# One gathered tile's rows spread over more chunks, and a short convolution read from PSUM, in a two-layer decoder trunk

## The reference, cut to what matters

```
xn = rms_norm(x);  lru_in, fox_qkv, ..., gate_in = split(xn @ w_in)
y  = causal depthwise convolution of lru_in, 4 taps:  y = xp[:, 0:S]*w[0] + b;  y += xp[:, k:k+S]*w[k]
r  = sigmoid(y @ wa + ba);  i = sigmoid(y @ wx + bx)            # blocks of 128
a  = exp(-8 r softplus(-lam));  u = sqrt(1 - a*a) * (i * y)
h  = scan: h[t] = a[t] h[t-1] + u[t]                            # ya
x  = x + (g0*(ya@Wa) + g1*(yb@Wb) + g2*(yc@Wc)) @ w_out         # yb forgetting attention, yc mLSTM

hn = rms_norm(x);  q = hn @ wq                                  # 8 heads, 2 halves of 128
s1, s2 = q1 @ sub1.T, q2 @ sub2.T;  v1,i1 = top16(s1);  v2,i2 = top16(s2)
top_s, pos = top16(all 256 sums v1+v2);  idx = i1*128 + i2      # 16 of 16384 experts per head
act = gelu(dot(u_tab[idx], hn));  x = x + sum softmax(top_s) * act * v_tab[idx]
```

## Time and profile before

| | us |
|---|---|
| median of 3 runs (lowest, highest) | 4760.27 (4757.66, 4764.66) |
| the profiled execution | 4777.11 |
| its span, first to last instruction | 4775.3 |
| PE busy / PEld / DVE / ACT / POOL | 4448.6 / 3691.8 / 3138.8 / 1810.5 / 2693.7 |
| granted TensorE clock, mean | 0.972 |

### The profile page before, as it was taken

The page is one execution under the profiler, slowest core; times in us unless marked ns, Lnnn a source line. Parts: engine busy times, 40 slices in busy tenths (PEclk is TensorE's granted clock), DMA queues, the critical chain, the costliest instruction groups (busy, mean ns, idle before and its releaser), DMA issues.

```text
span 4775.3 us, 73532 instructions
## 1 busy us (share of the span) xinstructions
PE 4448.6 (93%) x21322; PEld 3691.8 (77%) x21322; DVE 3138.8 (66%) x5007; ACT 1810.5 (38%) x3307; POOL 2693.7 (56%) x1477
## 2 busy tenths in 40 slices
PE   7999999999999998999989999999999898889998
PEld 5766775789889897777767667757898898877776
DVE  5754223448889776888867541244488897668888
ACT  2234114124566652333332341231245666533333
POOL 5743663665456675555558436636654566655554
PEclk9999999999999999999999999999999999999999
DMA  3211221224689999999822112212246899999997
GB/s 105 80 49 36 80 81 47 70 78 137 182 259 283 298 318 329 335 343 333 292 87 84 49 36 83 79 42 75 80 142 192 260 288 302 335 315 343 340 338 268
DMA packets 467060, 891.87 MB, mean 187 GB/s; under 512 B 45600, under 2 KB 324640, under 8 KB 463776
## 3 DMA queue, kind: packets, MB, share of 16 engines
q1 hardware_dynamic: 387424, 617.22, 40.1%
q0 software_dynamic: 73728, 268.47, 16.2%
q10 hardware_dynamic: 5696, 3.85, 0.3%
HBM read 786.61 MB, written 102.76 MB: 186 GB/s over the span
## 4 chain that ended last, share of the span: by engine, by line
PE 61%; DVE 12%; issue 11%; DMA 8%; POOL 3%; ACT 3%; SPq 1%; DVEq 0%; ACTq 0%; POOLq 0%; another core or an unknown queue 0%
PE pair L824 6%; DMA ring<-v_tab 5%; PE bank L1230 5%; PE bank L824 5%; PE bank L1235 5%; PE bank L1225 4%; PE bank L1173 4%; PE bank L850 3%; PE pair L850 3%; PE pair L826 3%; PE bank L826 3%; PE bank L990 2%; PE bank L1177 2%; DMA ring<-u_tab 2%; DVE qk L2329 1%
## 5 line engine op out<-in xcount | busy, mean ns | idle before, releaser
L678 POOL TENSOR_TENSOR w_hi<-ring,ones 128x1024 fp32r<-128x1024 f32 x272 | 536.4, 1972 | 844.8 <-PE bank L850 277.8
L666 POOL TENSOR_TENSOR w_lo<-ring,w_hi 128x1024 fp32r<-128x1024 f32 x256 | 615.8, 2406 | 539.8 <-ACT w_hi L1628 532.3
L1173 PE MATMUL bank<-xT,w_hi 128*128 128x384 f32 x2048 | 720.3, 352 | 40.0 <-ACT gst L1640 36.4
L681 POOL TENSOR_TENSOR w_lo<-ring,w_hi 128x1024 fp32r<-128x1024 f32 x272 | 693.8, 2551 | 21.3
L1173 PE MATMUL bank<-xl_peer,w_hi 128*128 128x384 f32 x2048 | 698.8, 341 | 0.0
L1634 ACT CAST w_hi<-ring 128x1024 fp32r<-128x1024 f32 x252 | 266.0, 1056 | 671.7 <-PE bank L1235 445.3
L1628 ACT CAST w_hi<-ring 128x1024 fp32r<-128x1024 f32 x256 | 269.6, 1053 | 598.6 <-DVE ring L2297 427.8
L2389 DVE TENSOR_TENSOR cl<-att,ch 128x384 fp32r<-128x384 f32 x256 | 354.8, 1386 | 172.6 <-ACT ch L1699 165.6
L672 POOL TENSOR_TENSOR w_lo<-ring,w_hi 128x1024 fp32r<-128x1024 f32 x126 | 301.8, 2395 | 280.5 <-ACT w_hi L1634 280.5
L1173 PEld LDWEIGHTS bank<-xT,w_hi 128*128 128x128 f32 x2048 | 397.3, 194 | 43.1 <-ACT w_hi L1628 34.6
L1225 PE MATMUL bank<-w_hi,ch 128*128 128x512 f32 x1524 | 392.1, 393 | 21.4 <-ACT ch L1699 21.4
(11 more groups left out here) (360 smaller groups left out, 9332.8 us busy)
## 6 DMA issues: line engine op xcount, KB each, us to landing
ring<-v_tab SPq DMA_DIRECT2D x252, 512.0 KB
ring<-w_stream SPq DMA_DIRECT2D x240, 512.0 KB
ring<-u_tab SPq DMA_DIRECT2D x512, 128.0 KB
g_spill<-gst SPq DMA_DIRECT2D x256, 192.0 KB
hn<-u_tab SPq DMA_DIRECT2D x256, 128.0 KB
x_last<-u_tab SPq DMA_DIRECT2D x256, 128.0 KB
w_spill<-vg SPq DMA_DIRECT2D x12, 2048.0 KB
w_spill<-att SPq DMA_DIRECT2D x12, 2048.0 KB
```

The costliest lines, as they stand in the source:

```text
L666: nc.gpsimd.tensor_tensor(w_lo[s % 2][:, :], ring[2 + s % 2][:, :], w_hi[s % 2][:, :].bitcast(F32), ALU.subtract)\
L678: nc.gpsimd.tensor_tensor(w_hi[b][:, 0:n], src, ones[:, 0:1].to_broadcast([P, n]), ALU.mult)\
L681: nc.gpsimd.tensor_tensor(w_lo[b][:, 0:n], src, w_hi[b][:, 0:n].bitcast(F32), ALU.subtract)\
L1173: nc.tensor.matmul(out, w_hi[s % 2][:, c * P:(c + 1) * P], dense_parts(c)[part], start=(c == 0 and part == 0), stop=False)
```

## The change

Two edits that don't touch each other.

**LRU.** ACT reads the slot from PSUM and makes the last tap (`last_tap`); DVE adds the other three from the same PSUM bank, slot by slot, shifted by 1, 2 and 3 columns; `xpad` is gone, the bank is drained when the third is added. `xc` and `TI` have a buffer for each block. FZ now comes before FV in the order of weights, and gate products 1 stand between slots 1 and 2 of FZ.

**The gathered tile.** In each of the first three query rounds DVE also does the last tile's best 16 of 256 sums for the round's two heads (`sparse_heads`), in place of doing it for all heads in UE. The experts of the first four heads follow in chunks 2 to 6 of UE, those of the rest in chunks 24 to 31; tile 0's choice moves to chunks 7 to 23 and tile 1's to 32 to 54. Gathers begin at chunk 8 and dots at chunk 12: 8 in chunks 11 to 23, 112 in 24 to 119, 8 in 120 to 127. 38 of the 128 dots (the first 8, then every fourth) are taken by two engines: POOL multiplies the row by the token's vector, of which DVE puts a copy in SBUF (`nwb`), and ACT sums (`row_sum`).

```diff
-ROWS = [0] * (4 * LEAD + 14) + shares(18, 18) + shares(40, 32) + shares(54, 32) + shares(16, 8) \
+ROWS = [0] * 11 + shares(8, 4 * LEAD - 11) + shares(112, 4 * WROUNDS) + shares(8, 8) \
     + [0] * 4 + shares(SLOTS, NCHUNK - 4)
+SHARED_ROWS = [n for n in range(SLOTS) if n < FIRST_ROW[4 * LEAD] or n % 4 == 3]
-        xc = merged[:, 0:4, :]
-        TI = og[:, 0:4, :]
+        xc = [merged[:, 0:4, :], yT[:, 4:8, :]]
+        TI = [og[:, 0:4, :], merged[:, 0:4, :]]
...
+            def row_times(L, n):
+                if n == SHARED_ROWS[0]:
+                    pool.wait_ge(row_ready.sem, row_ready.at(L, "N2", 0, 1))
+                pool.wait_ge(g_ready[n % NG], landed(L, n))
+                stand(pool)
+                nc.gpsimd.tensor_tensor(grow[n % NG], grow[n % NG], nwb[:, :], ALU.mult).then_inc(row_product.sem, 1)
...
                     if c < NCHUNK:
                         expert_low(L, c // 4, c % 4)
+                        for m in shared_rows(c):
+                            row_times(L, m)
-                    if c == 4 * LEAD + 11:
-                        pool.wait_ge(eidx_ready.sem, eidx_ready.at(L, "T", 0, 2))
+                    if c == 8:
+                        pool.wait_ge(eidx_ready.sem, eidx_ready.at(L, "T", 0, 1))
...
-                project_tokens(L, "FV", 0, of_tile(xT), xl_of_tile)
-                gate_products(1, range(2))
-                values = tokens_beside(L, "FV", 1, of_tile(xT), xl_of_tile, 24)
-                for _ in range(3):
-                    next(values)
-                gate_products(1, range(2, 4))
-                next(values)
-                values.close()
                 for s in range(4):
                     project(L, "FZ", 0, s, x_parts(xl_mix))
+                    if s == 1:
+                        gate_products(1)
+                for i in range(2):
+                    project_tokens(L, "FV", i, of_tile(xT), xl_of_tile)
...
-                def conv_input(i, s):
+                def last_tap(i, s):
+                    k = 4 * i + s
                     proj_wait(L, "LRU", i, s)
-                    nc.scalar.copy(xpad[:, 4 * i + s, CONV - 1:], bank[s][:, :]).then_inc(drained_sem[s], 1)
+                    nc.scalar.activation(xc[i][:, s, :], bank[s][:, :], ACT.Identity, scale=pcol("conv_w", (CONV - 1) * KC + k),
                                          bias=pcol("conv_b", k)).then_inc(tap_ready.sem, 1)
...
+                def row_sum(n):
+                    act.wait_ge(row_product.sem, row_product.at(L, "U", 0, shared_at(n)))
+                    nc.scalar.activation(grow[n % NG], grow[n % NG], ACT.Copy, accum_out=actv[:, n:n + 1])\
+                        .then_inc(row_summed.sem, 1)
...
+                def conv(i, s):
+                    k = 4 * i + s
+                    dve.wait_ge(tap_ready.sem, tap_ready.at(L, "LRU", i, s + 1))
+                    for back in range(1, CONV):
+                        ins = V.scalar_tensor_tensor(out=xc[i][:, s, back:], in0=bank[s][:, 0:SEQ - back],
+                                                     scalar=pcol("conv_w", (CONV - 1 - back) * KC + k), in1=xc[i][:, s, back:],
+                                                     op0=ALU.mult, op1=ALU.add)
...
+                        c = Chain(dve, heads_step, L, "WQ", i)
+                        for _ in sparse_heads(c, lambda j: slice_of(tv_s, i, j), lambda j: slice_of(posu_s, i, j)):
+                            pass
...
+                V.tensor_copy(nwb[:, :], pair[:, :]).then_inc(row_ready.sem, 1)
+                sooner, later = 1 + 8, 5 + 6 + 8 + 1
+                pieces = [[0] * 5 + shares(upto, 16) + [1], shares(sooner, 5)]
```

More of the change, by code:

```diff
@@ L1678, in _ @@
                     expert_high(0, s)
-                with act.Fori(0, LEAD - 2) as i:
+                with act.Fori(0, 2) as i:
                     round_of(i)
+                stand(act)
+                with act.Fori(0, 1):
+                    for i in range(2, LEAD - 1):
+                        round_of(i)
                 soft(0, wts)
-                round_of(LEAD - 2)
                 round_of(LEAD - 1, tile=0)
@@ L1690, in _ @@
                         round_of(LEAD + 8 * d + y, k=8 * d + y, tile=DENSE if y < 7 else d + 1)
-                with act.Fori(LEAD + WROUNDS, ROUNDS["UE"] - 1) as i:
-                    round_of(i)
+                stand(act)
+                with act.Fori(0, 1):
+                    for i in range(LEAD + WROUNDS, ROUNDS["UE"] - 1):
+                        round_of(i)
                 round_of(ROUNDS["UE"] - 1, last=True)
@@ L1887, in decay @@
                     dve.wait_ge(drained_sem[7], drained[7].at(L, "LRU", i, 2))
-                    dve.wait_ge(conv_done.sem, conv_done.at(L, "LRU", i, 4))
-                    ins = V.scalar_tensor_tensor(out=TI, in0=TI, scalar=1.0, in1=xc, op0=ALU.add, op1=ALU.mult)
+                    for s in range(4):
+                        dve.wait_ge(drained_sem[s], drnd(L, "LRU", i) + 2)
+                    ins = V.scalar_tensor_tensor(out=TI[i], in0=TI[i], scalar=1.0, in1=xc[i], op0=ALU.add, op1=ALU.mult)
                     if i == 0:
@@ new lines, in sparse_heads @@
+                def sparse_heads(c, best, where):
+                    v = kval.rearrange("p (h a t) n -> p t h a n", a=2, t=TT)[:, SP_T, :, :, :]
+                    both = cand[:, 0:2, :]
+                    pair_of = [P, 2, TOPK, TOPK]
+                    c.step(V.tensor_tensor(both.rearrange("p h (a b) -> p h a b", a=TOPK),
+                                           v[:, :, 0, :].unsqueeze(3).to_broadcast(pair_of),
+                                           v[:, :, 1, :].unsqueeze(2).to_broadcast(pair_of), ALU.add))
+                    c.wait()
+                    stand(dve)
+                    yield
+                    for n in range(2):
+                        for j in range(2):
+                            c.step(V.max(best(j)[n], both[:, j, :]))
+                        c.wait()
+                        stand(dve)
+                        yield
+                        for j in range(2):
+                            c.step(V.max_index(where(j)[n], best(j)[n], both[:, j, :]))
+                        c.wait()
+                        stand(dve)
+                        yield
+                        if n == 0:
+                            for j in range(2):
+                                c.step(V.match_replace(both[:, j, :], best(j)[n], both[:, j, :], NEG * 1e8))
+                            c.wait()
+                            stand(dve)
+                            yield
@@ new lines, in _ @@
+                for i in range(LAST):
+                    stand(dve)
+                    with dve.Fori(0, 1):
+                        c = Chain(dve, dve_step, L, "WQ", i)
+                        keys_wait(i)
+                        for _ in best_keys(c, i, 0, TT):
+                            pass
+                        dve.sem_inc(best_done.sem, 1)
+                        c.close()
+                        stand(dve)
+                        c = Chain(dve, heads_step, L, "WQ", i)
+                        for _ in sparse_heads(c, lambda j: slice_of(tv_s, i, j), lambda j: slice_of(posu_s, i, j)):
+                            pass
+                        c.close()
+                        stand(dve)
@@ L2366, in _ @@
                     for _ in range(ROWS[n]):
-                        dot(used)
+                        if used not in SHARED_ROWS:
+                            dot(used)
                         used += 1
@@ L2404, in _ @@
                     if n == 4:
-                        for _ in sparse_choice:
+                        for _ in second:
                             pass
```

294 lines of the change are left out of this document (162 added, 132 removed).

## The result

The changed kernel takes 4786.3 us (median of five runs, 4776.8 to 4794.4) against 4760.2 for the kernel before: a ratio of 1.0053, with a 95% interval of 1.0036 to 1.0071. It is slower by half a per cent; 4680 was forecast, with a range of 4630 to 4742. The profiled execution took 4794.4 with a span of 4792.5, 17.2 more than before.

The account below looks back on a forecast made before the run. PE is busy 4448.6 of 4775.3 us, so gains are PE's waits, in UE for DVE, later loads. 2 x 12.5 (LRU) - 2 x 4.5 (query rounds) + 35 + 29 (UE) = 80 us off 4760: 4680, range 4630 to 4742.

Parts of the forecast that it names:

- search 1 begins 1.2 us late and search 2 2.4: Query rounds: 6 us of heads against 4.78 us idle delay the searches; loss 4.5 us a layer, from 3 to 15.
- Chunks 54 to 87: 7 forecast: UE: DVE's sum of 5.29 us a chunk is over by 0.2, 7 us lost in layer 1, from 0 to 14.
- Behind a row product stands the next w_lo ... So I cost them at nothing there.: UE's weights chunks: POOL needs 4.4 and ACT 3.9 of 5.08 us a chunk, so shared rows cost PE nothing.
- Slower: Rival, UE: POOL and ACT wait on each other, shared rows hold w_lo beyond its cover; +100 us, 4860; chance 0.09.
- 1.05 us a row on: UE: the cost per shared row from which the slower rival decides, 76 rows against 80 us gained.
- 5 us of cover: UE's weights chunks: w_lo may be about 5 us late before PE notices.
- 2.4 us a row: UE, the slower rival: each row holding w_lo too long costs PE its product again; 76 x 2.4 = 182 us.
- 15 us a layer named for a thinner cover: UE's weights chunks: 0.5 us for each of 30 rows if w_lo's cover is thinner than taken.
- A chunk costs DVE's sum plus 0.35 us of small waits.: UE's weights chunks: DVE's work plus 0.35 us sets a chunk's time where that exceeds 5.08 us.
- the one at 25: UE, chunks 24 to 31: the start of the weights steps costs 5.5 us as before, within 15 forecast.
- the 1824 and 1557 KB a chunk: UE, chunks 88 to 119: loads per chunk before and after, put at 359 and 306 GB/s; the window moved 316.
- The rule weighed in the prediction: DVE with two SBUF inputs and GpSimd reading SBUF share ports in turn; if offloading didn't help, about 4740.

Follow-up runs that it names:

- e3_sum_first: The changed kernel with ACT's sum of a shared row put ahead of w_hi of the same step instead of behind it; ratio 0.9922 to the kernel before.
- e2_unshared: The changed kernel with only the first 8 rows shared, all 112 rows of the weights chunks being DVE's dots; ratio 0.9959 to the kernel before.
- e11_no_subtract: The changed kernel without DVE's subtraction of the maximum in the dense tiles' softmax, exp reading the scores themselves; ratio 1.0018 to the kernel before.

## Why the prediction was wrong, step by step

**LRU: right.** 12.5 us a layer forecast, 11.0 and 12.4 measured; the taps at 0.75 for 0.69, and the splits of POOL are late next.

**Query rounds: the mechanism right, the size half.** The work of the heads was sized well (6). The step that failed is "search 1 begins 1.2 us late and search 2 2.4": I set 6 against an idle time of 4.78 and left out the gaps around the heads (1.0 before the next search, 0.3 ahead), and a sum that can meet a split (2.46 us in place of 0.69). It cost 9.9 us in place of 4.5.

**UE: wrong, and here is nearly all of the miss,** 90 of the 97 us between the forecast gain of 80 and the 17 lost by the profiles. By its parts: chunks 0 to 24 right in sum (11; 12.0 and 12.4), but by some luck, since chunk 9 alone cost 4.0 and 3.8 us for the 1.7 forecast and chunk 0 lost 1.3 us more than before, its first matmuls starting every 0.32 us behind the longer wait; the surplus came out smaller. Chunks 24 to 53: 15 + 15 forecast, 42.5 and 38.8 measured. Chunks 54 to 87: 7 forecast, 28.6 and 31.3. Chunks 88 to 119: 6; 14.1 and 11.5. The last eight: 12; 15.4 and 15.6.

Two steps failed.
- "Behind a row product stands the next w_lo ... So I cost them at nothing there." I compared POOL's and ACT's sums with the chunk's 5.08 us, and both were right: the product took 2.39 and the sum 1.05 + 0.18, as estimated. What cost was the order. The sum stood behind an operation that waits for DVE, and four things stood behind the sum. By e3_sum_first the place of the sum alone is worth 27 us a layer, 0.7 us for each of the 38 shared rows. The rival "Slower" had the ring of three engines and its point of decision, "1.05 us a row on", but looked for it at w_lo and its 5 us of cover; the rows show it at the scaled one-hots, which have none, and PE waits for w_lo in the whole run 13.4 us, nearly all of it in chunks 9 to 24. Its 2.4 us a row was too much, and the 15 us a layer named for a thinner cover too little. So the kernel is slower, but not by that rival's mechanism.
- "A chunk costs DVE's sum plus 0.35 us of small waits." With the order mended (e3), chunks 88 to 119 lose 7.2 and 5.6, as forecast, and chunks 32 to 53 lose 20.1 and 21.1 for 15. But chunks 54 to 87 lose 20.1 and 19.4 and not 7. Even e2_unshared, with 0.45 us a chunk more for DVE, loses about the same (18.4 and 21.5). By the ends of single chunks the loss is no rate: in layer 1, the chunks that lose over 2.5 us hold 75 of 100 us before (11 chunks), 77 of 111 in the changed kernel (15) and 55 of 84 in e3_sum_first (10). Three of them are where a tile's weights begin. Chunk 25 loses 4.9 to 5.5 us in the three kernels in layer 1, chunk 57 6.0, 4.9 and 5.0, chunk 89 4.2, 4.1 and 2.5. The prediction had the one at 25 and took the rest for DVE's rate. The rate was also got from unequal stretches, tile 2's choice over 30 chunks against a window of 34; over all 34 DVE's sum is 5.33 us, and 0.52 are left over it, not 0.35. In chunk 57 PE waits for the scaled one-hots, 3.2 us in all three kernels, and the rest is about what the lower clock behind that wait costs (granted over the chunk: 0.69, 0.83, 0.83); what makes the one-hots late there was not tried. Without the subtraction it costs 1.8 us in layer 1 and 5.0 in layer 2. Chunk 76 loses another 6.6 and 5.8 us in e3_sum_first, of which the cause is open too.

A slip that decided nothing: the 1824 and 1557 KB a chunk are of 1024 bytes, so in 5.08 us they are 368 and 314 GB/s, not 359 and 306, and 314 is no longer clearly below the 316 that the window moved. With the order mended the window of chunks 88 to 119 moved 298 and lost about what was forecast.

**What was asked of the profile.** The wait of w_hi for the transpose fell from 427.8 to 339.3 us in the whole run, a fifth and not the half. PE's waits for w_lo appear at chunks 9 to 24 as foreseen; two of under 0.3 us come later. DVE's waits for u_tab behind chunk 87 stayed at 30 us in place of 15:

```profile
DVE ring L2423 <- DMA ring<-u_tab: 30.4, 4, 19.4
```

Of these, 19.4 us are chunk 124's, which has the same 2 MB ahead of it with half the rows.

**The rule weighed in the prediction.** DVE's dots kept their 1.219 us beside POOL's products, so these operations, with an input in PSUM, are not slowed, as argued. The rows of the subtraction show the other side: with both inputs in SBUF, a subtraction of 128x128 elements took up to 5.2 us beside two POOL operations. The Trainium skill (SBUF — State Buffer, Who interferes with whom) has this as an exclusive lock on the shared pair of ports; the trace agrees, and shows in addition that DVE waits through POOL's second operation when the two follow each other without a gap (4.79, 5.19, 4.82 and 5.21 us in four of six cases). The warning of the Trainium skill (Perfetto Trace Analysis, Optimizing Scalar/DVE Operations) that an offload to GpSimd might not help was right in its effect: e2_unshared is 42 us better in UE without it. The reason is mostly another. Removing the subtraction, where the port shows, gave 19 us (e11_no_subtract), mending the order 54, and with the order mended the offload does help: 164.3 against 175.9. The two gains don't add, since with the order mended the removal gave 0.8.

## What to carry to other kernels

Work taken off the busiest engine is free on another only if the place in that engine's order is free: ask what the new instruction stands behind, and what stands behind it, before its sum is compared with the period. Put it ahead of the instruction at which that engine idles, not behind; here that alone took the kernel from 0.5% slower to 0.8% faster. A loss that is fitted as a rate should be split by chunks first: here more than half of it stood in a dozen of them, and chunks 25 and 57 lost about the same with DVE's load a chunk 0.45 us higher or lower (e2_unshared, e3_sum_first).
